# Hybrid decoder layer on one Trainium2 core: eight of 24 projection eighths moved from the first half of a linear-attention head to its second, and v transposed five slots later

## What is computed

```
def step(state, inp):
    qi, ki, vi, gi = inp
    cum = cumsum(gi)
    o_inter = (qi * exp(cum)) @ state
    decay = where(causal, exp(cum_i - cum_j), 0)
    scores = sum_k qi[i,k] * ki[j,k] * decay[i,j,k]
    state = state * exp(last) + (ki * exp(last - cum)).T @ vi
    return state, o_inter + scores @ vi
o = rms_norm(o, gla_out_norm_g) * silu(gla_r)
```

## Time and profile before

| | |
|---|---|
| median of 3 runs | 2291.52 us |
| lowest and highest run | 2288.26 and 2295.66 us |
| the profiled execution's own time | 2295.39 us |
| its span, first to last instruction | 2293.4 us |
| TensorE matmul busy over the span | 2131.7 us (93%) |
| VectorE, ScalarE, GpSimd busy | 1287.4, 757.0, 921.2 us |
| mean granted TensorE clock | 0.967 of 2.4 GHz |

### The profile page before, as it was taken

How to read it: one execution, slowest core, us unless ns; L and a number is a source line. 1 busy time by engine, 2 the same in 40 slices (tenths; PEclk the granted TensorE clock), 3 DMA queues, 4 the chain that set the end, 5 groups by cost and what they waited for, 6 DMA issues and landing times. The chain is left out here.

```text
span 2293.4 us, 29780 instructions
## 1 busy us (share of the span) xinstructions
PE 2131.7 (93%) x10088; PEld 1724.4 (75%) x10088; DVE 1287.4 (56%) x1744; ACT 757.0 (33%) x1326; POOL 921.2 (40%) x733
## 2 busy tenths in 40 slices
PE   4999989998999999999999699997799999999999
PEld 3787777777877777777877478886688888888887
DVE  4557676852275675675676466557544444444444
ACT  3223232321154454454454420002422222223322
POOL 3322222222244344344344233332855555555552
PEclk7999999999899999999999799998799999999999
DMA  3211111222414314314324172221111111111111
GB/s 104 48 34 46 28 46 30 49 48 78 99 29 101 78 41 101 78 41 101 78 41 110 70 270 74 91 83 46 56 56 44 37 47 55 55 55 55 55 55 73
DMA packets 137775, 153.84 MB, mean 67 GB/s; under 512 B 7664, under 2 KB 112112, under 8 KB 137728
## 3 DMA queue, kind: packets, MB, share of 16 engines
q1 hardware_dynamic: 136000, 150.07, 23.8%
q10 hardware_dynamic: 1728, 3.15, 0.4%
HBM read 107.06 MB, written 20.97 MB: 56 GB/s over the span
## 5 line engine op out<-in xcount | busy, mean ns | idle before, releaser
L123 POOL TENSOR_TENSOR w_hi<-w_raw,w_ones 128x64 fp32r<-128x64 f32 x88 | 34.2, 389 | 763.7 <-PE gla_g L147 362.2
L478 POOL TENSOR_TENSOR sb_rows<-sb_beta,sb_rest 128x128 f32<-128x128 f32 (+7 forms) x128 | 166.1, 1302 | 250.8 <-DVE sb_rest L833 250.8
L833 DVE TENSOR_TENSOR_SCAN sb_rest<-sb_rest 128x128 f32<-128x128 f32 (+7 forms) x128 | 205.6, 1614 | 33.6 <-ACT sb_beta L684 33.6
L126 POOL TENSOR_TENSOR w_lo<-w_raw,w_hi 128x1024 fp32r<-128x1024 f32 x88 | 218.5, 2483 | 7.3
L839 DVE TENSOR_TENSOR sb_wt_lo<-sb_t,sb_wt_hi 128x512 fp32r<-128x512 f32 x192 | 106.4, 554 | 172.3 <-ACT sb_wt_hi L692 170.3
L692 ACT CAST sb_wt_hi<-sb_t 128x512 fp32r<-128x512 f32 x192 | 92.6, 482 | 234.0 <-PE sb_t L577 232.8
L147 PE MATMUL sb_g<-h_hi,w_hi 128*128 128x512 f32 x544 | 161.1, 421 | 3.7 <-DVEq L737 3.7
L147 PE MATMUL sb_g<-h_lo,w_hi 128*128 128x512 f32 x544 | 156.3, 413 | 0.0
L147 PE MATMUL sb_g<-h_hi,w_lo 128*128 128x512 f32 x544 | 153.1, 406 | 0.0
L147 PE MATMUL gla_g<-h_hi,w_hi 128*128 128x512 f32 x480 | 132.1, 408 | 1.8 <-DVEq L1251 1.8
L577 PE MATMUL sb_t<-ident,sb_rows 128*128 128x128 f32 x576 | 102.4, 289 | 32.1 <-DVE sb_wt_lo L839 32.0
(11 more groups left out here) (310 smaller groups left out, 5084.6 us busy)
## 6 DMA issues: line engine op xcount, KB each, us to landing
w_raw<-w_in SPq DMA_DIRECT2D x64, 512.0 KB, 8.1
ff_raw_g<-w_ffn_gate SPq DMA_DIRECT2D x11, 1024.0 KB, 5.4
ff_raw_u<-w_ffn_up SPq DMA_DIRECT2D x11, 1024.0 KB, 5.8
ff_raw_d<-w_ffn_down SPq DMA_DIRECT2D x11, 1024.0 KB, 4.9
sb_qs<-sb_q_st SPq DMA_DIRECT2D x32, 256.0 KB, 5.1
sb_kh<-sb_k_st SPq DMA_DIRECT2D x32, 256.0 KB, 5.1
sb_kl<-sb_k_st SPq DMA_DIRECT2D x32, 256.0 KB, 5.0
mp_sig<-gates_t SPq DMA_DIRECT2D x16, 512.0 KB, 4.4
```

The source lines that it names most:

```text
L123: self.nc.gpsimd.tensor_tensor(hi[:, 0:64], raw[:, 0:64], self.ones[:], ALU.mult)
L126: self.nc.gpsimd.tensor_tensor(lo, raw, hi, ALU.subtract).then_inc(self.ready, 1)
L478: nc.gpsimd.tensor_tensor(rows[tb // 4][:, tb % 4, 0:width], beta[:, n % 2, 0:width], rest[:, n % 2, 1:width + 1], ALU.mult).then_inc(row_ ...
L833: nc.vector.tensor_tensor_scan(back, back, back, 1.0, ALU.mult, ALU.bypass).then_inc(scanned, 1)
```

## The change

Three lists give the number of eighths in each slot. In slots 0 to 23 a slot has one eighth, except slots 1, 4, 7, ..., which have none; in slots 24 to 47 a slot has one, except slots 25, 28, ..., which have two. That is 16 and 32 eighths instead of 24 and 24, in the same order of units. GLA_HALF holds the slot after the one that completes a half: 6, 12, 18, 24, 27, 30, 33, 36, 39, 42, 45, 48 in place of 4, 8, ... 48. The copies of q, k, vt, r and the gates stand at these slots. The transposes and copies of v move from slots 33 to 36 to slots 38 to 41. The place of every other operation stays.

```
+GLA_FILLS = [(s % 3 != 1) if s < 24 else 1 + (s % 3 == 1) for s in range(GLA_SLOTS)]
+GLA_FIRST = [sum(GLA_FILLS[:s]) for s in range(GLA_SLOTS)]
+GLA_HALF = [next(s for s in range(GLA_SLOTS) if GLA_FIRST[s] + GLA_FILLS[s] > 4 * n + 3) + 1 for n in range(2 * GLA_UNITS)]
+GLA_VT = range(38, 42)
...
 TensorE:
-                            if s in (33, 34, 35, 36):
-                                if s == 33:
+                            if s in GLA_VT:
+                                n = GLA_VT.index(s)
+                                if n == 0:
                                     for half in range(NH):
                                         pe.wait_ge(g_free[half], g_uses(it) + 5)
-                                transpose_v(s - 33, t_uses(it) + CHUNKS + 4 + s - 33)
-                        fill(GLA_UNITS * it, GLA_UNITS + s // 8, s % 8, g_uses(it) + s // 8)
+                                transpose_v(n, t_uses(it) + CHUNKS + 4 + n)
+                        for f in range(GLA_FIRST[s], GLA_FIRST[s] + GLA_FILLS[s]):
+                            fill(GLA_UNITS * it, GLA_UNITS + f // 8, f % 8, g_uses(it) + f // 8)
...
 ScalarE:
-                            if s in (20, 24, 28, 32):
-                                i = (s - 20) // 4
+                            if s in GLA_HALF[4:8]:
+                                i = GLA_HALF[4:8].index(s)
...
-                            if s in (33, 34, 35, 36):
-                                copy_v(s - 33, t_uses(it) + CHUNKS + 4 + s - 33)
+                            if s in GLA_VT:
+                                n = GLA_VT.index(s)
+                                copy_v(n, t_uses(it) + CHUNKS + 4 + n)
...
-                            if s in (36, 40, 44):
-                                i = (s - 36) // 4
+                            if s in GLA_HALF[8:11]:
+                                i = GLA_HALF[8:11].index(s)
...
-                        elif s >= 4 and s % 4 == 0:
-                            i = s // 4 - 1
+                        elif s in GLA_HALF:
+                            i = GLA_HALF.index(s)
...
 VectorE:
-                            if s in (4, 8):
-                                copy_q(s // 4 - 1, g_uses(it))
-                            if s in (12, 16):
-                                copy_k(s // 4 - 3, g_uses(it) + 1)
+                            if s in GLA_HALF[0:2]:
+                                copy_q(GLA_HALF.index(s), g_uses(it))
+                            if s in GLA_HALF[2:4]:
+                                copy_k(GLA_HALF.index(s) - 2, g_uses(it) + 1)
```

## The result

The changed kernel takes 2317.39 us (median of six runs, 2310.34 to 2323.02) against 2291.52: a ratio of 1.0111, interval 1.0093 to 1.0129, so 25.9 us or 1.1% slower. The profiled execution took 2314.01 us, span 2312.0. The prediction said 2308.4 and 2299 to 2321, with 87% on slower: the direction and the range held, the size was 16.9 us where 25.9 were measured.

A forecast was written before the change was run, and what follows sets the result against it. A latency loop through VectorE was taken to bound each head's first 24 slots, with TensorE almost filled. 3 x 3.4 + 9.5 - 2.8 = +16.9 us gave 2308.4 us; likeliest 2303 to 2316, widened to 2299 to 2321.

The forecast's parts named there:

- The first half: First 24 slots: eight eighths leave, chunk loop stays 7.76 us, TensorE idles more; saved 0, bounds 0 and 1.31 per chunk.
- The last head: Last head's end: no preparation, one moved eighth fills part of the 3.12 us wait, seven are added; +9.5 us.
- Heads 0 to 2: Last 24 slots of these heads: eight added eighths partly fill waits; each head grows 3.4 us, bounds 1.3 and 6.
- The copies of k: VectorE's copies of q and k at slots 6, 12, 18, 24: short, behind the reduce, cover kept; cost 0.
- The copies of V: Slots 38 to 41: copies queue behind exponentials on ScalarE, 2.1 us of waiting in place of 1.74, bounds 0 and 5.
- The walk: Step-by-step timing of head 1's last 24 slots, bringing TensorE to 353.4 without V-copy waits, 355.5 with them.
- The clock: Head starts of heads 1 and 3: without idle stretches before them, full clock returns about 2.8 us.
- rival D: First half: idling lowers the clock, 1.6 us for each of 31 later chunks; +67 us, 2358; 6%.
- rival B: Last 24 slots: the next head's preparation becomes the bound, 3 us more per head; +26 us, 2317.4; 12%.
- Rival A: Last 24 slots: added eighths meet no waits of their own, +1.3 per head; +10.6 us, 2302.1; 20%.
- Rival C: First half: the loop is TensorE's after all, each of 32 chunks shrinks by 1.31; -25 us, 2266.5; 5%.

The follow-up runs named there:

- x1_loop: Changed kernel, but in the first 24 slots the slot without an eighth is the one behind the outputs (2, 5, 8, ...); 2272.37 us, ratio 0.9909.
- x8_place: Changed kernel with 24 and 24 eighths, later v kept, the eighth behind the outputs issued before them (1, 2, 0 per chunk); 2272.80 us, ratio 0.9916.
- x3_last: Changed kernel, but the last head has one eighth in each slot as before; 2312.75 us, ratio 1.0086.
- x5_k: Changed kernel, with the second copy of k behind the normalisation (slot 25) instead of ahead of it (slot 24); 2310.92 us, ratio 1.0091.
- x4_half: Changed kernel, but only four eighths move (slots 1, 7, 13, 19 have none; 25, 31, 37, 43 two); 2288.54 us, ratio 0.9978.
- x6_vspace: Changed kernel, with transposes and copies of v in slots 38, 40, 42, 44 instead of 38 to 41; 2315.48 us, ratio 1.0101.
- x9_alt: Changed kernel, but four eighths move instead of eight, and no slot behind the outputs has an eighth; 2262.24 us, ratio 0.9866.

## Why the prediction was right, and where it was not

**The first half, right.** "Each leaves from between scores and outputs, so out of the cover and not out of the loop": the period stayed within 0.1 us and the wait grew by 42 us in 32 chunks. x1_loop and x8_place show the loop itself: in the first the eighth behind the outputs is taken out, and the period falls by 1.30 us, the 1.31 of the prediction; in the second it is put beside VectorE's work. The -0.08 us per chunk was not foreseen.

**The last head, right.** Seven eighths uncovered, +9.5 us predicted and measured, and the wait for obuf fell from 3.12 to 1.79 us, by the one eighth that was to fill it; x3_last gave 6.7 us back in the medians and 8.0 in the profile.

**Heads 0 to 2, right in mechanism and too small.** The term was 3.4 us a head and measured 6.0, so 18.1 us for the three where 10.2 were forecast. The copies of k were costed at nothing, "their cover is kept, so 0": for the second half of k this failed. Slot 24 is ahead of the gate weights and the normalisation on VectorE, and VectorE waits there for TensorE. I put the first vt transpose 36.8 to 37.3 us behind chunk 7's start; it came at 38.0 in head 1 and 39.1 in heads 0 and 2, and with that copy moved (x5_k) at 37.1 in all three, inside the range. So x5_k prices the copy of k at 1.2 us a head, and at 2.0 where the slow stretch behind the logits came with it: 5.1 of the 7.9 us. The copies of V, forecast 1.3, 0.7 and 0.1 us late (2.1 in all), came 2.1 and 0.5 late in heads 0 and 2. In head 1 the 2.1 us were followed by a stretch of the lower clock: from there to the next head were 19.6 us against 18.5 in the other two, although the second wait is missing. These two make most of what is left.

The walk itself has two slips. The "four transposes of 0.5 us in all" must be 0.5 us each for its 353.4 to come out. And not two splits but three fell into the preparation already before: they start at 320.19, 338.35 and 349.23 us, and VectorE was busy with it from 317.91 to 351.93 us.

**The clock, wrong in size.** I took 2.8 us back for head starts without idle time. The first periods of heads 1 to 3 gave 1.4 (26.25 us to 24.83), since head 2 now began slowly. The rule of the Trainium skill, TensorE: Matmul & The Clock Gate, A second HAM failure mode, was not borne out for the case that I weighed: none of the 28 chunks with 1.45 us of idling was followed by the lower clock, so rival D's price of 50 us was not paid. The 1.6 us of one chunk were paid once, in the first chunk of head 2, where the idling was 1.96 us. Over the changed kernel, x3_last, x4_half, x5_k and x6_vspace, 4 of 19 such first chunks were followed by the lower clock, and none of 117 chunks with 1.43 to 1.50 us. Elsewhere a shorter wait goes with it: of nine logits that waited 0.3 us (changed kernel, x3_last, x6_vspace) seven were followed by the lower clock, and none of the 24 in the kernel before and the other runs, where the logits did not wait. What starts a stretch stays open: the same waits come with and without one.

**The preparation, not the bound.** It took 35.3 us of VectorE where it had taken 34.0, and VectorE was done 2.6 us before TensorE in head 1, so rival B's mechanism did not decide. That B's total, 2317.4 us, is the measured one is a coincidence: B had the end of the preparation as the bound, and the time lies in the late copies of k and V and in the clock. Rival A, no new waits, falls with the 7.3 us for V and the logits. Rival C falls with the period of 7.67.

So 7.9 us too little for heads 0 to 2 and 1.4 too much of regained clock make 9.3 us; the shorter reduce gives 2.0 back, and 16.9 becomes 24.2.

## What to carry to other kernels

A short wait that is there in every iteration marks a latency loop. Work can be added beside such a loop for nothing up to its latency, and taken away there gains nothing; only what stands in the loop counts, and often it can be issued one place earlier. Before moving work to fill idle time, add up that idle time: here the waits of a head's second half came to 7.2 to 9.0 us, four eighths (5.4 us) fitted and eight (10.9 us) did not. And when a copy moves later, read what its engine has queued behind it.

## What was not expected of the hardware

VectorE's reduce of 1024 elements took 1.91 us in each chunk where TensorE stood still during most of it, and 1.99 in the kernel before and in x1_loop, where TensorE worked. In x4_half, where every second chunk is without an eighth, the two alternate, 1.90 to 1.95 us and 1.98 to 2.02. What lies between the two engines was not tested.

GpSimd's split slows even operations of eight elements per partition: single ones took 2.21 and 2.25 us instead of 0.17. Every operation on these small tiles that took over 0.25 us, in all eleven profiles, overlapped a split; in x4_half and x9_alt no split fell there, and none took longer than 0.25.
